# The q projection blocks of a hybrid encoder step run inside the streams' latent attention

## The reference, cut to what matters

```python
z = jnp.einsum("bld,dn->bln", hn, w_in)
qa, ka, va, cq, dkv, ga, gb = jnp.split(z, IN_SPLITS, axis=-1)
oa = diff_attention(qa, k_all, v_all, ...)              # differential attention: q, k, v projections, 1024 columns each
ob = mla_attention(q_nope, q_pe, k_nope, kr_all, v, ...) # latent attention, from cq and dkv
m = jax.nn.sigmoid(ga) * oa + jax.nn.sigmoid(gb) * ob
h = h + jnp.einsum("bld,de->ble", m, w_out)
```

## Time and profile before

| what | before |
| --- | --- |
| time, median of 3 runs | 3091.91 us (3090.02 to 3093.69) |
| time of the profiled execution | 3103.5 us |
| its span, first to last instruction | 3101.3 us |
| PE busy | 2778.4 us, 90% |
| DVE busy | 1468.1 us, 47% |
| ACT busy | 943.1 us, 30% |
| POOL busy | 253.6 us, 8% |
| mean granted PE clock | 0.919 of 2.4 GHz |
| chain of waits: share of PE | 78% |

### The profile page before, as it was taken

One profiled execution on the slowest core, in us unless ns is written; L12 is line 12 of the kernel. 1 busy time (PEld: TensorE's weight loads), 2 busy tenths in 40 slices (PEclk: granted clock), 3 DMA queues, 4 the chain that ended last, 5 costly groups with the idle time before them and its releaser, 6 DMA issues.

```text
span 3101.3 us, 53162 instructions
## 1 busy us (share of the span) xinstructions
PE 2778.4 (90%) x17464; PEld 2539.0 (82%) x17464; DVE 1468.1 (47%) x2602; ACT 943.1 (30%) x2032; POOL 253.6 (8%) x684
## 2 busy tenths in 40 slices
PE   5888899889889899999988888996987998999996
PEld 5865599767689899999978557995776998999996
DVE  5635221234453674655657332113445346737366
ACT  3324223344421331222232331233453113313132
POOL 3100100110000010100001010001000001101010
PEclk8979599889999899999999876997998998999998
DMA  4210024421122222222223001334111222222222
GB/s 122 51 45 0 22 68 120 136 64 44 41 54 67 61 74 68 75 68 75 61 64 66 10 5 45 85 111 136 45 41 42 68 68 60 67 78 71 69 69 78
DMA packets 376793, 201.27 MB, mean 65 GB/s; under 512 B 66438, under 2 KB 368636, under 8 KB 376658
## 3 DMA queue, kind: packets, MB, share of 16 engines
q1 hardware_dynamic: 346722, 178.99, 20.7%
q10 hardware_dynamic: 25344, 12.27, 1.3%
q0 software_dynamic: 4592, 8.35, 0.9%
HBM read 183.84 MB, written 17.88 MB: 65 GB/s over the span
## 4 chain that ended last, share of the span: by engine, by line
PE 78%; DVE 6%; issue 5%; ACT 4%; DVEq 3%; DMA 2%; ACTq 1%; SPq 1%; POOL 0%; POOLq 0%
PE ps L536 21%; PE ps L540 20%; PE ps L537 20%; PE ps L676 1%; PE ps L703 1%; PE ps L633 1%; DMA k_past<-in_cache_a_k 1%; DVE rstd L1604 1%; ACT w_hi L1144 1%; PE ps L864 1%; PE ps L575 1%; PE ps L863 1%; PE ps L578 1%; PE ps L844 1%; PE ps L701 1%
## 5 line engine op out<-in xcount | busy, mean ns | idle before, releaser
L536 PE MATMUL ps<-hn_hi,w_hi 128*128 128x328 f32 x2848 | 884.8, 317 | 6.1 <-DVE w_lo L1586 3.7
L537 PE MATMUL ps<-hn_lo,w_hi 128*128 128x328 f32 x2848 | 875.4, 313 | 0.0
L540 PE MATMUL ps<-hn_hi,w_lo 128*128 128x328 f32 x2848 | 661.3, 314 | 0.0
L1586 DVE TENSOR_TENSOR w_lo<-w_raw,w_hi 128x1024 fp32r<-128x1024 f32 x300 | 367.0, 1224 | 545.1 <-ACT w_hi L1144 540.2
L1144 ACT ACTIVATE w_hi<-w_raw 128x1024 fp32r<-128x1024 f32 x300 | 316.8, 1058 | 833.0 <-PE ps L540 629.8
L536 PEld LDWEIGHTS ps<-hn_hi,w_hi 128*128 128x128 f32 x2848 | 536.5, 188 | 22.5 <-issue 19.7
L537 PEld LDWEIGHTS ps<-hn_lo,w_hi 128*128 128x128 f32 x2848 | 537.2, 189 | 0.2
L540 PEld LDWEIGHTS ps<-hn_hi,w_lo 128*128 128x128 f32 x2848 | 484.1, 188 | 0.0
L536 PE MATMUL ps<-s_hi,w_hi 128*128 128x328 f32 x704 | 221.7, 321 | 18.8 <-DVE w_lo L1586 14.2
L537 PE MATMUL ps<-s_lo,w_hi 128*128 128x328 f32 x704 | 221.2, 319 | 0.0
L540 PE MATMUL ps<-s_hi,w_lo 128*128 128x328 f32 x704 | 167.5, 320 | 0.0
(11 more groups left out here) (333 smaller groups left out, 4230.3 us busy)
## 6 DMA issues: line engine op xcount, KB each, us to landing
w_raw<-in_w_in SPq DMA_DIRECT2D x98, 512.0 KB
w_raw<-in_w_up SPq DMA_DIRECT2D x88, 512.0 KB
w_raw<-in_w_down SPq DMA_DIRECT2D x32, 512.0 KB
out<-tok_out ACTq DMA_DIRECT2D x32, 256.0 KB, 2.3
k_past<-in_cache_a_k SPq DMA_DIRECT2D x16, 512.0 KB, 5.4
v_past<-in_cache_a_v SPq DMA_DIRECT2D x16, 512.0 KB, 3.4
w_raw<-in_w_a_br SPq DMA_DIRECT2D x16, 512.0 KB
w_raw<-in_w_out SPq DMA_DIRECT2D x16, 512.0 KB
```

What stands on the lines that cost most here:

```text
L536: mm(dst[:, c, :], w_hi[:, slot, k, :], x_hi[:, k, cols], start=(k == 0), stop=False)
L537: mm(dst[:, c, :], w_hi[:, slot, k, :], x_lo[:, k, cols], start=False, stop=False)
L540: last = mm(dst[:, c, :], w_lo[:, slot, k, :], x_hi[:, k, cols], start=False, stop=(k == nk - 1))
L1586: tt(w_lo[:, slot], w_raw[:, slot], w_hi[:, slot].bitcast(F32), ALU.subtract).then_inc(w_split[slot], 1)
```

## The change

The eight q blocks leave their `job` and go into the latent loop, one block a stream, in four parts of two contraction tiles (12 matmuls each): after the keys, after the turn, after the scores and after the values. On PE this is `query_part`. The q results use other PSUM banks (`q_acc`: `tq` for slot 0, banks 2 and 3 for slot 1), and the stream's output moves from `tq` to bank 1 (`c_out`). ACT empties a q block in the next stream's turn (`query`), after that stream's weight split; DVE's weight splits stand ahead of its score work. SP's loop over the streams is unrolled, and the q weights are loaded in pairs between the cached rows. PE's wait for `ob_done` now stands directly between the `uv` products and the first k block. `qT` and the buffers of the differential stage get new places in SBUF, and `d_e` becomes two tensors.

```diff
-        qT, kT = run(R1, ("qT", [P, KD, T]), ("kT", [P, KD, T]))
-        oa_hi, = run(R1, ("oa_hi", [P, KD, T], F32R))
+        v_tok, kT, v_meta = run(R1, ("v_tok", [P, QT, D]), ("kT", [P, KD, T]), ("v_meta", [META, D]))
+        ob_hi, ob_lo, oT_new, qT = run(
+            Z, ("ob_hi", [P, 4, T], F32R), ("ob_lo", [P, 4, T], F32R), ("oT_new", [P, H, P + META]),
+            ("qT", [P, KD, T]))
+        oa_hi, = run(names["qT"][0], ("oa_hi", [P, KD, T], F32R))
+        oa_lo, = run(names["ob_hi"][0], ("oa_lo", [P, KD, T], F32R))
...
+        q_acc = (ps[:, 4:6, 0:HALF], ps[:, 2:4, 0:HALF])
+        c_out = ps[:, 1, 0:KC * P]
...
# SP
-                load(l, B_Q, 0, KD, qkv(0))
+                for j in range(2):
+                    load(l, B_Q + j, 0, KD, qkv(j))
...
-                with e.Fori(0, STREAMS // 4) as i:
+                for i in range(STREAMS // 4):
                     for half in range(2):
...
+                        if i or half:
+                            for j in range(2):
+                                pair = 2 * i + half
+                                load(l, B_Q + j, pair, KD, qkv(2 * pair + j))
-                load(l, B_Q + 1, 0, KD, qkv(1))
-                columns(B_Q, 3 * KD // 2 - 1, lambda t, j: (KD, qkv(t)), first=1)
+                columns(B_Q, 3 * KD // 2 - 1, lambda t, j: (KD, qkv(t)), first=KD // 2)
...
# PE
-                        dst = tq[:, 0, c * P:(c + 1) * P]
+                        dst = c_out[:, c * P:(c + 1) * P]
...
+                def query_part(i, k, part):
+                    b = B_Q + k
+                    slot = b % 2
+                    if part == 0:
+                        block_ready(l, b, i * 2)
+                    for kt in range(2 * part, 2 * part + 2):
+                        last = product(slot, kt, KD, hn_hi, hn_lo, out=q_acc[slot])
+                    if part == 3:
+                        last.then_inc(block_done[slot], 1)
...
                         if k < 4:
                             latent_keys(i, k)
+                            query_part(i, k, 0)
                         if k:
                             latent_turn(step - 1, True)
                         if k < 4:
+                            query_part(i, k, 1)
                             e.wait_ge(cs["keys"], l * STREAMS + i * 4 + k + 1)
                             latent_scores(step, 0, SKEYS)
+                            query_part(i, k, 2)
                         if k:
                             latent_values(step - 1, k - 1, True)
+                        if k < 4:
+                            query_part(i, k, 3)
...
                 e.wait_ge(cs["out_done"], (l + 1) * (STREAMS + 1))
+                for s in range(2):
+                    e.wait_ge(acc_free[s], uses(l, s, (B_K - s + 1) // 2))
...
-                job(l, B_Q, KD // 2, KD, hn_hi, hn_lo)
                 e.wait_ge(ob_done, l + 1)
...
# ACT
+                def query(i, k):
+                    s = arrived(l, B_Q + k, i * 2)
+                    act(halves(one(qT[:, ds(i * 4 + k, 1), :])), q_acc[s], ACT.Copy).then_inc(acc_free[s], 1)
+
+                split(l, B_Q + 1)
                 with e.Fori(0, STREAMS // 4) as i:
...
                         if k:
+                            split(l, B_Q + k + 1, i * 2)
+                            query(i, k - 1)
                             latent_turned(step - 1, k - 1, True)
...
-                job(l, B_Q, KD // 2, lambda t, s: act(halves(one(qT[:, ds(t, 1), :])), accs(s), ACT.Copy).then_inc(acc_free[s], 1))
...
-                    split(l, (B_K, B_V)[what] + j + 1, i)
+                    if what or j or not isinstance(i, int):
+                        split(l, (B_K, B_V)[what] + j + 1, i)
...
-                        last = act(d_e[:, n % 2, g, 0:nk], d_e[:, n % 2, g, 0:nk], ACT.Exp, bias=negmax[:, g:g + 1], accum_out=sums[:, g:g + 1])
+                        last = act(d_e[n % 2][:, g, 0:nk], d_e[n % 2][:, g, 0:nk], ACT.Exp, bias=negmax[:, g:g + 1], accum_out=sums[:, g:g + 1])
...
# DVE
+                split(l, B_Q + 1)
                 with e.Fori(0, STREAMS // 4) as i:
                     for k in range(5):
                         step = l * (STREAMS + 1) + i * 4 + k
+                        if k:
+                            split(l, B_Q + k + 1, i * 2)
                         if k < 4:
                             latent_scores(step, SKEYS)
...
-                job(l, B_Q, KD // 2, None)
```

More of the change, by code:

```diff
@@ L181, in build @@
         c_past, kr_past, c_mn = run(ZX, ("c_past", [P, 4, KV_LORA]), ("kr_past", [P, 4, ROPE]), ("c_mn", [P, KV_LORA]))
-        c_keyT, kr_keyT, qa_s, qpe_s, c_e, c_eT, c_eT2 = run(
+        c_keyT, kr_keyT, qa_s, qpe_s, c_e, c_eT = run(
             names["kbT"][0], ("c_keyT", [P, KC, SKEYS]), ("kr_keyT", [P, SKEYS]), ("qa_s", [P, KC, P]),
-            ("qpe_s", [P, P]), ("c_e", [P, SKEYS]), ("c_eT", [P, P]), ("c_eT2", [P, P]))
-        qT, kT = run(R1, ("qT", [P, KD, T]), ("kT", [P, KD, T]))
@@ L188, in build @@
-        oa_hi, = run(R1, ("oa_hi", [P, KD, T], F32R))
+            ("qpe_s", [P, P]), ("c_e", [P, SKEYS]), ("c_eT", [P, P]))
+        c_eT2, = run(names["c_mn"][1], ("c_eT2", [P, P]))
+        v_tok, kT, v_meta = run(R1, ("v_tok", [P, QT, D]), ("kT", [P, KD, T]), ("v_meta", [META, D]))
+        ob_hi, ob_lo, oT_new, qT = run(
+            Z, ("ob_hi", [P, 4, T], F32R), ("ob_lo", [P, 4, T], F32R), ("oT_new", [P, H, P + META]),
+            ("qT", [P, KD, T]))
+        assert names["qT"][0] >= names["c_eT"][1]
@@ L203, in build @@
+        pdT, q_bd, d_e0 = run(names["v_meta"][0], ("pdT", [P, 2, H, 2 * DEC]), ("q_bd", [P, H, 2 * DEC]),
+                              ("d_e0", [P, 2, SKEYS]))
+        d_e = (d_e0, d_e1)
+        assert names["d_e0"][1] <= Z
         assert names["keyT"][0] >= names["tok_out"][1]
@@ L956, in new_turn @@
                         if past:
-                            mm(tq[:, 0, g * 64:(g + 1) * 64], d_e[:, n % 2, g, 0:PAST], mixer[:, g, :], start=True, stop=True)
-                        last = mm(tq[0:rows, 0, P + g * 64:P + (g + 1) * 64], d_e[:, n % 2, g, PAST:SKEYS] if past else d_e[:, n % 2, g, 0:META], mixer[:, g, :], start=True, stop=True)
+                            mm(tq[:, 0, g * 64:(g + 1) * 64], d_e[n % 2][:, g, 0:PAST], mixer[:, g, :], start=True, stop=True)
+                        last = mm(tq[0:rows, 0, P + g * 64:P + (g + 1) * 64], d_e[n % 2][:, g, PAST:SKEYS] if past else d_e[n % 2][:, g, 0:META], mixer[:, g, :], start=True, stop=True)
                     last.then_inc(dn["pturned"], 1)
@@ L1900, in _, with keys_copied @@
                 tt(ob_lo[:, :, META:NEW], obT[:], ob_hi[:, :, META:NEW].bitcast(F32), ALU.subtract).then_inc(ob_done, 1)
-                job(l, B_Q, KD // 2, None)
-                with e.Fori(0, KD // 2) as i:
-                    for j in range(2):
-                        split(l, B_K + j + 1, i)
+                def keys_copied(i, j):
                         e.wait_ge(stage_ready[j], l * KD + i + 1)
@@ L1908, in _ @@
                         copy(one(kT[:, ds(i * 2 + j, 1), :]), stage[:, j]).then_inc(k_copied[j], 1)
+                keys_copied(0, 0)
+                split(l, B_K + 2)
+                keys_copied(0, 1)
+                with e.Fori(1, KD // 2) as i:
+                    for j in range(2):
+                        split(l, B_K + j + 1, i)
+                        keys_copied(i, j)
                 job(l, B_V, KD // 2, None)
```

31 lines of the change are left out of this document (13 added, 18 removed).

## The result

The changed kernel takes 3048.68 us (median of 4 runs, 3043.57 to 3059.43) where the kernel before took 3090.97 beside it: a ratio of 0.9857, 95% interval 0.9838 to 0.9876. That is 42 us less. The forecast was 34 us less: 3058, range 3034 to 3084. A second set of six runs of the same kernel gave 3057.72 (3050.28 to 3066.45) against 3094.0, ratio 0.9883, 0.9859 to 0.9907: 36 us less.

A forecast was written before the change was run, and what follows sets the result against it. TensorE's time was taken as the bound, with waits and half clock in the latent loop. Terms summed to 117.8 us a layer against 134.8, 34.0 less over two layers: 3058 us, range 3034 to 3084.

The forecast's parts named there:

- eight streams: Latent loop: each stream with its q block takes 11.3 us (7.22 + 0.44 + 3.6), 90.1 us a layer.
- two round ends: At `k` = 4 PE waits 2.0 us for ACT's split, emptying and copies, twice: 4.0 us a layer.
- a dip at a round end: After a round's end PE may fall to half clock: one dip counted, 1.5 us a layer, bounds 0 and 3.0.
- late weights of the fifth block: The fifth q block's load follows the second round's cached rows: nothing counted, 2 us as upper bound.
- the wait for `ob_done`: Between `uv` and the k blocks PE stands 3.4 us a layer, no longer covered by q blocks.
- start of the k blocks: After that wait the k blocks start at half clock: 1.8 us a layer, bounds 1.0 to 2.9.
- the latent steps: A stream's attention work on PE falls from 6.4 us at half clock to 3.6, bounds 3.2 and 4.1.
- the part entries: Each of a q block's four parts has a slower first contraction tile: 0.11 us a part, 0.44 a block.
- the rival of 0.06: The loop's clock stays at half: 64 us a layer lost, median 3219; chance 0.06.
- The point of decision: A fifth of the streams' work at half clock (17.0 of 84 us) decides whether the change becomes slower.
- ACT's queue: Rival: splits or copies late in every stream; at 2 us a stream the gain is eaten, about 3091; chance 0.10.
- the rival of a loss behind the stage: New memory in the differential stage costs about what the change gains: 3085 to 3100 us; chance 0.04 (nothing gained).

The follow-up runs named there:

- e5: The changed kernel run once more, unchanged: 3057.72 us.
- e3: The changed kernel with each stream's q block in one piece behind the values: 3115.68 us, ratio 1.0070 to the kernel before.
- e8: e2 with the same four q blocks whole, in four parts, in every second stream and none in the others: 3070.68 us, ratio 0.9922.
- e2: The changed kernel with half a q block in each stream, four blocks left behind `uv`: 3041.29 us, ratio 0.9827.
- e9: e3 with unread extra transposes in front of each of a stream's two waits, PE's wait for weights and banks ahead of them: 3091.8 us, ratio 0.9986.
- e6: e4 with, at `k` = 4, ACT copying turned probabilities before split and emptying, and DVE's split behind its stream work: 3043.61 us, ratio 0.9846.
- e4: The changed kernel with the prompt's latent outputs split in four pieces inside the latent loop: 3042.44 us (one run).
- e1: The changed kernel's new memory places and bank kept, q blocks back behind `uv`: 3098.77 us, ratio 1.0015 to the kernel before.
- e10: e3 with ACT copying the turned probabilities ahead of its split and emptying, leaving only the keys' wait: 3081.43 us, ratio 0.9964.
- e7: e2 with tiles in the round ends, two blocks among meta rows and `uv`, two behind, ACT's turned copies first at `k` = 4: 3014.28 us, ratio 0.9738.

## Why the prediction was right, and where its terms were off

The direction, the mechanism and the range held: 3058 was forecast, 3048.68 and 3057.72 are the two medians. By the stage the gain is 45.2 us in the first profile and 41.0 in the second (149.1 - 131.7 and 149.1 - 125.5), where 34.0 was forecast: the medians lie nearer to the forecast than the stage does, which is the spread of the other stages and no merit of the sum. Term by term, layer 1 of the first profile:

| term | forecast | measured |
|---|---|---|
| eight streams | 90.1 | 85.0 (8 x 10.63) |
| two round ends | 4.0 | 4.3 (2 x 2.14) |
| start at half clock | 1.8 | at most 2.0 (0.12 of 17 us) |
| a dip at a round end | 1.5 | 0; in e5 3.3 |
| late weights of the fifth block | 0 | 0.17 |
| meta rows and `uv` | 15.2 | 14.6 (405.37 to 419.97) |
| the wait for `ob_done` | 3.4 | 4.0 (3.99, to 423.96) |
| start of the k blocks | 1.8 | 2.6 (423.96 to 441.03, less 14.44) |
| sum | 117.8 | 112.9 (313.69 to 441.03, less 14.44); the terms give 112.7 |

**The term that was off is the stream**, by 0.63 us of 11.26, eight times: 5.0 of the 4.9 us. It has two halves. First, the latent steps. I took 57% of their time at half clock for all of them, from a row with a pause between tiles of 128 and of 32 rows. That ratio holds for the values alone, which have such pauses: 2.89 us before (four groups of 0.72), now 0.41 to 0.43 a group, 1.66. Keys and turn went from 1.25 to 0.55, scores from 2.24 (327.06 to 329.30) to 1.01: 45%. Together 3.22, forecast 3.6. A ratio from one kind of step was laid over steps of another kind. Second, the part entries. Only where a part follows the scores is its first product longer, 0.34 against 0.15 in the chain above; behind transposes it is 0.15 like all others. That is 0.19 us a stream where 0.44 was counted. The row of `diff_prompt` that I used for all four entries has scores ahead of it too.

**The clock.** It went to 1.00 in the loop as forecast, and the rival of 0.06 did not come. But its mechanism is real, and nearer than I had thought: e3 has the same work with 1.6 us of waits in 12.5 and lost 8 us a layer against the kernel before, and e8 lost 16 against e2. The point of decision that I gave, a fifth of the streams' work at half clock, no run tests by itself: e3's loss has about as much of longer streams in it as of clock. I argued the clock from how much PE works; e9 shows that what counts in these streams is that PE does not wait. The Trainium skill ("TensorE: Matmul & The Clock Gate", section "A second HAM failure mode: psum-queue depth-cycling") puts such a swing, seen there in a bf16 kernel, down to short idles of PE between groups of matmuls; e3, e8 and e9 agree, with clocks of 0.82, 0.66 to 1.00 in turn, and 0.98 once the idles are filled.

**The covered key waits** are the other half of the mechanism, and the two can't be added up: the parts between the steps take away the waits, and with them the reason for the low clock. e2 says how much was needed for it, half a block a stream.

**ACT's queue** did not become the bound: behind the fifth block's late weights PE waited 0.17 us, in the streams between not at all. Those weights used up nearly all of the slack: ACT's split of them began 5.2 us into the fourth stream (350.48; I had reckoned with 4.5). Only at the round ends did the split and the emptying stand in the way, as counted, and e6 took that out.

**The wait that moves** was counted with its length and its slow start, 3.4 + 1.8; in layer 1 they were 4.0 and 2.6, and it is luck that the meta rows and `uv` came out 0.6 shorter. e4 gained 4.9 us in layer 1 and 2.9 in layer 2, the shorter wait and the quicker start together; e6 shows that the quicker start does not always come with it.

**The differential stage** kept its length (263.9 and 259.3 us after, 267.6 and 265.6 in e1, 266.0 and 265.9 before, within the spread of executions), so the rival of a loss behind the stage falls too.

What stays open: why a round's end is followed by a dip in one execution and not in another, and when one wait a stream is enough to bring the clock down (e10). The length of a wait does not settle it. At the end of the first round 2.14 us were followed by a dip in one of two layers of e5 and in none of the first profile, e4 and e9, while the 0.84 us of e2 were followed by one in both layers (the 0.83 of its second row) and those of e6 in none.

## What to carry to other kernels

Where PE waits again and again for short copies at half clock, put independent products into the waits, in pieces as long as the waits: e3 and the kernel after do the same work, 29 and 31 us a layer apart. Put in no more than the waits need, and keep the rest for the next chain of waits: that is the step from the kernel after to e7, 43 us. And measure the stage from anchor to anchor, since the rest of the kernel moves by 10 us between executions.

## What the runs showed of the hardware

Seven transposes that nobody reads, in front of each wait, cost no time in e3's streams (12.5 us at full clock with and without them) and made the stage 15 us shorter in the profiled executions (156.6 to 141.3 on average over the layers), by the clock. In the loop before, PE was busy 84% of the time and still at 0.50; in e3, where it was busy 92.5 of 107 us, the clock moved between the levels, mean 0.82; in e7, without idle time from 320 us on, it stayed at 1.00 with small fp32 matmuls and products mixed.
